# RWKV-7 rounds: four pieces of work moved behind steps of the state chain, and one product in place of two

## What is computed

```
def step(S, inp):
    rt, wt, kt, vt, kkt, at = inp
    sa = einsum('rbhvk,rbhk->rbhv', S, -kkt)
    S = S * wt[..., None, :] + sa[..., None] * (kkt * at)[..., None, :] + vt[..., None] * kt[..., None, :]
    return S, einsum('rbhvk,rbhk->rbhv', S, rt)
```

## Time and profile before

| what | us |
| --- | --- |
| median of 3 runs (2269.49 to 2280.86) | 2274.34 |
| the profiled execution | 2281.17 |
| its span, first to last instruction | 2279.4 |
| PE busy in the span | 1958.1 |
| DVE busy | 1063.6 |
| POOL busy | 696.6 |
| ACT busy | 602.9 |

### The profile page before, as it was taken

The page is one execution under the profiler, slowest core; times in us unless marked ns, Lnnn a source line. Parts: engine busy times, 40 slices in busy tenths (PEclk is TensorE's granted clock), DMA queues, the critical chain, the costliest instruction groups (busy, mean ns, idle before and its releaser), DMA issues. The chain is left out here.

```text
span 2279.4 us, 50850 instructions
## 1 busy us (share of the span) xinstructions
PE 1958.1 (86%) x21128; PEld 1819.7 (80%) x21128; DVE 1063.6 (47%) x1874; ACT 602.9 (26%) x1330; POOL 696.6 (31%) x550
## 2 busy tenths in 40 slices
PE   5599797989199748878887369999999999999998
PEld 3589796777199737767776259999999999999998
DVE  7604544565622374444543874533333434334354
ACT  4313342111111245554553022411020101101024
POOL 4303330010224352231221232234344343434450
PEclk8799898898599989999999579999999999999999
DMA  9554010000211000000000140011111111211122
GB/s 324 152 164 153 19 37 5 3 0 1 101 37 37 25 5 4 7 4 4 4 3 4 31 124 6 28 38 56 46 28 46 37 46 37 55 38 36 46 56 84
DMA packets 147375, 110.04 MB, mean 48 GB/s; under 512 B 13182, under 2 KB 144277, under 8 KB 146709
## 3 DMA queue, kind: packets, MB, share of 16 engines
q1 hardware_dynamic: 147221, 107.74, 15.5%
HBM read 93.17 MB, written 14.55 MB: 47 GB/s over the span
## 5 line engine op out<-in xcount | busy, mean ns | idle before, releaser
L251 PE MATMUL banks<-Z_r 128*128 128x384 f32 x2016 | 352.3, 335 | 0.0
L251 PEld LDWEIGHTS banks<-Z_r 128*128 128x128 f32 x2016 | 349.3, 188 | 2.0 <-issue 0.9
L2547 DVE SCALAR_TENSOR_TENSOR XT<-banks,MOD,XT 128x128 f32 x224 | 110.8, 515 | 227.6 <-PE banks L251 226.8
L2881 ACT ACTIVATE PAD<-banks 128x384 f32<-128x384 f32 x96 | 47.2, 492 | 505.6 <-PE banks L2776 505.4
L2997 DVE TENSOR_TENSOR PAD<-PAD 128x384 f32<-128x384 f32 x96 | 98.7, 1028 | 143.2 <-ACT PAD L2881 143.0
L233 POOL TENSOR_TENSOR Z_r<-Z,ones 128x512 fp32r<-128x512 f32 x56 | 76.9, 1373 | 257.3 <-DMA Z<-in_mlp_w 257.3
L2776 PE MATMUL banks<-HT_r,W_r 128*128 128x384 f32 x768 | 149.1, 335 | 2.6 <-ACT HT_r L2848 1.6
L233 POOL TENSOR_TENSOR W_r<-Z,ones 128x1024 fp32r<-128x1024 f32 x32 | 77.0, 2406 | 239.8 <-DMA Z<-in_mlp_w 239.6
L2776 PE MATMUL banks<-YT_r,W_r 128*128 128x384 f32 x768 | 148.6, 334 | 0.0
L2776 PE MATMUL banks<-HT_r,Z_r 128*128 128x384 f32 x768 | 148.5, 334 | 0.0
L2776 PEld LDWEIGHTS banks<-HT_r,W_r 128*128 128x128 f32 x768 | 134.4, 188 | 3.5 <-issue 1.9
(11 more groups left out here) (411 smaller groups left out, 4198.5 us busy)
## 6 DMA issues: line engine op xcount, KB each, us to landing
Z<-in_w_mod SPq DMA_DIRECT2D x16, 1024.0 KB, 5.1
Z<-in_mlp_w SPq DMA_DIRECT2D x32, 512.0 KB, 4.3
Z<-in_mlp_w SPq DMA_DIRECT2D x58, 256.0 KB, 2.9
YT<-in_w_in SPq DMA_DIRECT2D x18, 512.0 KB, 3.9
XT<-in_w_mod SPq DMA_DIRECT2D x8, 1024.0 KB, 10.7
residual<-Z SPq DMA_DIRECT2D x1, 4608.0 KB, 17.8
low_part<-XT_r SPq DMA_DIRECT2D x1, 4608.0 KB, 15.4
XT<-residual SPq DMA_DIRECT2D x3, 1536.0 KB, 10.5
```

The lines of the kernel that those rows point to most:

```text
L251: mm = nc.tensor.matmul(self.bank(slot, g), w[slot][:, k, :], x(k, g), start=(n == 0 and k == 0), stop=(n == 2 and k == self.blocks - 1))
L2547: ins = nc.vector.scalar_tensor_tensor(out=x, in0=S.PS[3 * slot + g][:, a:b], scalar=S.MOD[:, ds(col, 1), c:c + 1].rearrange("p a b -> p ( ...
L2881: nc.scalar.activation(R[slot][:, grp(g)], up.bank(slot, g), ACT.Relu).then_inc(up.drained[g].sem, 1)
```

## The change

On ACT, K's factor moves from the head of a round to the place behind the first copies of q and u. On POOL, the K product moves from the head of the round behind the seeds, and the seeds wait for the chain's first new state. On DVE, the K rows move from the place ahead of step 0 of the chain into step 1, behind its new state (in the opening round behind two masked products). The decay of the state becomes one product over both directions instead of two; for this POOL stores the ends of the backward direction in reverse order. No matmul and no instruction of PE is changed.

```
     def round_act(act, chain, nxt, after, par):
         r, n, a = chain, nxt, after
+        if r is not None:
+            q_act(act, r, 0)
+            u_act(act, r, 0)
         if n is not None:
             tok = direction_tiles(act, n)[0]
             for d in range(2):
                 ka_act(act, n, d, tok[d])
         if r is not None:
-            q_act(act, r, 0)
-            u_act(act, r, 0)
             q_act(act, r, 1)
             u_act(act, r, 1)
...
-        for d in range(2):
-            ins = nc.vector.tensor_tensor(C.S[:, d, :, :], C.S[:, d, :, :],
-                                          C.ends[par][:, d, :, chunk(d, j)].unsqueeze(2).to_broadcast([P, NP, N]), ALU.mult)
-        ins.then_inc(f["new_state"].sem, 1)
+        ends = C.ends[par].rearrange("p d q j -> p (d q) j")[:, :, j]
+        nc.vector.tensor_tensor(heads(C.S), heads(C.S), ends.unsqueeze(2).to_broadcast([P, 2 * NP, N]),
+                                ALU.mult).then_inc(f["new_state"].sem, 1)
...
-            for d in range(2):
-                k_rows_dve(dve, n, d)
         if r is not None:
             state_dve(dve, r, par, 0, tiles, first if n is not None else None)
...
+        def k_rows():
+            for d in range(2):
+                k_rows_dve(dve, n, d)
+
         if r is not None:
-            state_dve(dve, r, par, 1, tiles)
+            state_dve(dve, r, par, 1, tiles, k_rows if n is not None else None)
+        elif n is not None:
+            k_rows()
...
     def r_rows_pool(pool, a, d, par, tok):
-        nc.gpsimd.tensor_copy(C.ends[par][:, d, :, :], C.EP[:, d, :, :, end]).then_inc(f["ends"].sem, 1)
+        ends = C.EP[:, d, :, :, end]
+        nc.gpsimd.tensor_copy(C.ends[par][:, d, :, :], ends[:, :, ::-1] if d else ends).then_inc(f["ends"].sem, 1)
...
     def round_pool(pool, chain, nxt, after, par):
         if n is not None:
-            tok = direction_tiles(pool, n)[0]
-            for d in range(2):
-                k_dir_pool(pool, n, d, tok[d])
...
             done(pool, "unit_l", n, 2)
+            if r is not None:
+                done(pool, "new_state", r, 1)
...
                     done(pool, "seeded", n, 2 * d + h + 1)
+            tok = direction_tiles(pool, n)[0]
+            for d in range(2):
+                k_dir_pool(pool, n, d, tok[d])
```

## The result

| kernel | median us | ratio to before [95% interval] |
| --- | --- | --- |
| before | 2276.90 | |
| after | 2315.07 (2304.74 to 2323.24) | 1.0169 [1.0116, 1.0223] |

What follows compares the result with a forecast made beforehand. No engine was full; PE's waits in a chain across engines were taken as the bound. -6.5 - 9.7 - 7.9 + 28.5 + 2.0 + 1.8 + 16.0 = +24.2 us gave 2298 us, range 2279 to 2313.

Steps and rivals of the forecast that it cites:

- K's factor: On ACT, K's factor behind q and u: PE's ten waits for q's copy shorten to 0.58 each, 6.5 us gained.
- Seeds, K product, one decay: POOL's seeds and K product behind the new state, one decay product on DVE: PE's nine decay waits shorten, 9.7 us gained.
- Clock behind the second q run: With shorter idle before PE's second q run, its clock rises from 0.50 to 1.00: 6 x 1.31, 7.9 us gained.
- The three gains: The terms -6.5 (K's factor), -9.7 (seeds, K product, decay) and -7.9 us (clock behind the second q run).
- Wait of tanh: ACT's tanh waits for the later K rows, delaying the grown copies and PE's level 1: 28.5 us lost over seven rounds.
- The first rival: Tanh's wait for the K rows doesn't bind, only the gains remain: -24.1, 2250 us, faster; 7%.
- Round 7 and the opening round: Level 1 starts later there: 2.0 us lost in round 7, 1.8 in the opening, plus 1.3 each for half speed.
- the sum: All terms of the prediction added up: +24.2 us on the profiled execution's 2281.2 us.
- The clock behind the new wait: PE idles some 3.9 us before level 1, then runs at half speed: 2.1 us a round, 16.0 lost in all.
- The clock stays up: Rival: tanh's wait binds but no half speed follows it; +6.9, 2281 us, within 0.5%; 15%.
- Half speed at both places: Rival: the second q run stays at 0.50 too; 2306 us, or 2315 with a third stretch each round; 13%.
- What the profile would show: Signs: ACT idle 5 to 7 us before tanh, PE about 4 before level 1, full rounds of some 47 to 48 us.

Runs made afterwards that it cites:

- factor_back: rows_ahead with K's factor put back at the head of ACT's round; 2266.26 us, ratio 0.9978.
- seeds_free: opening_back without GpSimd's wait for the first new state, so seeds follow the unit matrices at once; 2257.32 us, ratio 0.9933.
- two_products: opening_back with the decay as two products, one for each direction; 2254.60 us, ratio 0.9908.
- rows_alone: The kernel before with only the K rows moved behind the second new state; 2321.59 us, ratio 1.0242.
- rows_ahead: The changed kernel with the K rows put ahead of step 1 of the chain, the rest kept; 2250.37 us, ratio 0.9927.
- two_buffers: The changed kernel with decay buffer CS held twice, so tanh waits only for K rows of the tile before the last; 2282.51 us, ratio 1.0044.
- filled_third: The changed kernel with four unused matmuls, in place of filled_wait's twelve, in PE's idle behind the state step; 2303.27 us, ratio 1.0136.
- opening_back: rows_ahead with the opening round put back as in the kernel before; 2248.91 us, ratio 0.9907.
- filled_wait: The changed kernel with twelve unused matmuls in PE's idle behind the state step of each full round; 2289.42 us, ratio 1.0089.

## Why the prediction was right in its mechanism and wrong in its size

- **K's factor, -6.5.** Right: PE's waits for q's copy fell by 6.6 (12.3 to 5.7). factor_back prices the move at 9.8 in a kernel without other losses, since half speed follows the longer wait there in three rounds.
- **Seeds, K product, one decay, -9.7.** Right: 21.8 to 12.1 is 9.7. Not all parts count alike: the seeds' wait for the state is worth 5.3 of it (seeds_free), one product in place of two 0.6 (two_products); the remaining 3.8 was not tried alone. rows_alone shows 4.1 by a way that the prediction does not name: the K rows leave the place ahead of step 0, and the seeds come earlier. So the split depends on the order in which the parts are undone.
- **Clock behind the second q run, -7.9.** Right: from that run to u's copy took 4.00 us in round 5 (1132.48 to 1136.48) where it took 5.31. The three gains, sorted by place, come near the 20.3 us of rows_ahead, in part by luck as said there. The Trainium skill's rule (TensorE: Matmul & The Clock Gate, section Why this matters for your kernels), which warns only of longer idle gaps, would have had no gain here and no half speed in two_buffers and filled_third. The traces say otherwise.
- **Wait of tanh, +28.5.** Right: 7.65 at full speed instead of 7.46, 1.3 in seven rounds. The first rival (the wait doesn't bind) is out; it became true only when the K rows were put ahead of step 1.
- **Round 7 and the opening round.** Within 0.2 of the sum, in the opening round in part by luck: behind a wait of 2.26 us for a grown copy half speed lasted 10.1 us (845.3 to 855.4), where 1.3 had been priced from a stretch of 6.7; against it stand 3.4 us of half speed in before (882.6 to 886.0) that after does not have and the sum did not count.
- **The clock behind the new wait, 2.1 a round: this step failed.** The prediction took the length of the half-speed stretch from round 1 of before, 6.7 us, and allowed a cost of 3.4 us a round at most. That stretch stood behind an issue gap of 1.09 us (945.9), not behind a wait of 3.9. Measured: in the piece up to the masked product 9.06 - 7.65 = 1.41 in each of seven rounds, 9.9; in the piece behind it 210.2 against the 189.5 of opening_back, which is at full speed, 20.7. Together 30.6 us, where 14.7 was expected. That is 15.9 of the 18.2 us by which the rounds missed the sum; 1.3 more is the wait's own, and 1.0 lies between the adds, where issue gaps take 5.8 us instead of 4.8. The price of a microsecond at half speed was right: 2.1 for 6.7 us is 0.31, and 30.6 for the 104.8 us of the seven stretches is 0.29 (less in round 0, where 6.7 us of it cost 1.4). What was wrong is how long the clock stays low.
- **Rivals.** "The clock stays up" was given 2281; filled_wait, which nearly does that, is 13 above it by its ratio (+20 instead of +7). The pieces show 8.4 of this (330.5 against 315.4 + 6.7): 3.6 between the adds, 3.0 in the next, 1.8 behind. Issue gaps between the adds account for the first (8.4 us against the 4.8 of before), the longer wait and three full rounds that still have half speed for the others. "Half speed at both places" is out: the second q run is at 1.00.
- **What the profile would show.** As listed but for two sizes: ACT stood still 7.2 to 8.3 us ahead of tanh, not 5 to 7, and the full rounds took 49.6 to 51.5 us, not 47 to 48.

**Open.** What ends a half-speed stretch was not found. Behind the same 3.91 us it lasted 6.7, 13.5 and five times about 17 us, in rows_alone behind 3.98 us 7 to 17. The work that follows is the same at least from round 1 on (between rounds 0 and 1 the states are exchanged). That half speed follows the standstill is shown by filling it; its length is only measured.

## What to carry to other kernels

Before moving work behind a step, follow every semaphore that it signals to whoever overwrites its input, and on that engine to what is queued behind; here two instructions of 1.0 us in all put ACT's tanh and grown copies, and with them TensorE, behind a step that had hidden them. A standstill of TensorE can cost its own length and then the half speed behind it, here as much again (30.6 us against 7 x 7.65 - 23.6 = 30.0); price that by the longest stretch that the work behind could spend at half speed, not by one seen behind a shorter wait. Moves that gain together can lose apart: K's factor late on ACT pays only if the GpSimd work that waits for it no longer stands ahead of something urgent.

## What the runs showed of the hardware

Half speed came behind standstills of TensorE of 1.50 us (factor_back, three of seven rounds), 1.98 (two_buffers) and 2.04 (filled_third), all shorter than the 2.35 that had cost nothing in round 1 of before; behind 1.34 it did not come in the seven full rounds of rows_ahead. It came, too, behind an issue gap of 1.09 us in round 1 of before and of two_products, and behind one of 1.71 in seeds_free; the same 1.71 in round 5 of rows_ahead did nothing. So the idle time just before is not enough to tell whether the clock falls. Twelve matmuls a round whose result nobody reads made the changed kernel faster, 1.0089 against 1.0169 of before.
